# Scores of the bidirectional scan by pairs of heads, one sum of both directions ahead of the values, and an output-projection chunk asked for earlier

## The chip, the cores and the metric

The kernel runs on one core of one Trainium2 chip. The metric is the device time of one launch, in microseconds (us); lower is better. A core has a matrix engine (PE, with its weight loads shown apart as PEld), a vector engine (DVE), a scalar engine (ACT), GpSimd (POOL), and a queue engine (SP) that here does nothing but ask for transfers. They run on their own and meet at semaphores.

## The reference

Two layers (`DEPTH = 2`) over 256 latent tokens and 256 context tokens, 1024 wide. A layer has modulation vectors from two conditioning vectors, a normed and modulated input, one input projection whose columns feed four branches, one output projection, and then a mixture of 32 experts, two per token. All is float32. The branch that matters here is a gated linear attention with 4 heads (32 wide for queries and keys, 64 wide for values), in chunks of 64 tokens, once forward and once backward:

```python
def gla_chunked(q, k, v, log_a, s0):
    ...
    b = jnp.cumsum(log_a, axis=3)
    b_last = b[:, :, :, -1:, :]
    q_dec = q * jnp.exp(b)
    k_inv = k * jnp.exp(-b)
    mask = np.tril(np.ones((GLA_CHUNK, GLA_CHUNK), dtype=bool))
    scores = jnp.where(mask, jnp.einsum('bhnid,bhnjd->bhnij', q_dec, k_inv), 0.0)
    o_intra = jnp.einsum('bhnij,bhnjv->bhniv', scores, v)
    chunk_kv = jnp.einsum('bhnjd,bhnjv->bhndv', k * jnp.exp(b_last - b), v)
    ...
    o_inter = jnp.einsum('bhnid,nbhdv->bhniv', q_dec, s_in)
    return (o_intra + o_inter).reshape(bsz, nh, length, dv), s_final

def gla_bidir(q, k, v, la_f, la_b, s0_f, s0_b):
    o_f, s_f = gla_chunked(q, k, v, la_f, s0_f)
    rev = lambda t: jnp.flip(t, axis=2)
    o_b, s_b = gla_chunked(rev(q), rev(k), rev(v), rev(la_b), s0_b)
    return o_f + rev(o_b), s_f, s_b
```

The values `v` are the same for both directions, and the two outputs are added. In the last layer only the latent tokens go on after the scan.

## The kernel before

**Stages.** Each layer is written out once per engine. First the modulation products (`mod_product`, L1219), the norm, and the input projection with the local branches (L1259 to L1357); then the scan over token tiles of 128 (four tiles in layer 0, two in layer 1); then the router, and a loop over blocks of 32 tokens that stay with one expert (`expert`, L1584), while SP streams each expert's three chunks of 2 MB from memory (`refill`, L811).

**The scan stage.** `gla_steps` (L136) writes its order by hand, and PE, ACT and DVE all follow that list. For a tile `t` it has:
- `scores` (L1389): for each direction `d` one product, with `kiT` (the keys, 128 rows: 4 heads of 32, by 128 tokens) as the weights and `qbd` as the moving side. `qbd` is 128 x 512: the queries once per head with the rows of the other heads set to zero, which POOL writes (L917 to L924), a buffer for each direction, rewritten for the next tile once the scores of this tile are made.
- `masked` (L1838), on DVE: it reads the bank of each direction, multiplies by that direction's mask and writes `scm`.
- `outputs` (L1396): four products with the states (L1403), then for each direction and head one product of `scm` with the values (L1408), eight in all, summed in one bank. It waits once, for tile 0, on `s_S`: DVE signals that after `masked(0)` and the 14 steps of the state recurrence (L1852).
- `rows`, `ty` (L1382): norm and gate of the output, and its transpose.
- `pre` and `out` (`project_local`, `project_scan`; both through `product`, L1417): the output projection of the local branches and then of the scan's rows. `product` waits for both chunks of the projection weight, `wout` 0 and `wout` 1.

Every PE result goes through one of eight banks; `open_` (L1205) waits until the bank's last readers are done.

**The stream of weights.** `stream` (L259) is the list of 2 MB chunks that SP asks for in this order: `win` (input projection), `mod` (modulation), `wout`. `stream_slots` (L269) says which of four slots each goes to. Before each request SP waits for the landing of the chunk two places before it, and for the last use of what the slot held (L746 to L753), so a request that waits holds back every one behind it. Each `mod` chunk is used by one product of 16 matmuls.

Of the kernel before, what the change touches and what calls it, by code (L numbers as in the profile page):

```python
# [6 lines left out]
ALU = mybir.AluOpType  # L7
# [7 lines left out]
P = 128  # L15
D = 1024
KT = D // P
DEPTH = 2
# [7 lines left out]
HEADS = 4  # L26
DV = GROUP_W // HEADS
DK = DV // 2
# [43 lines left out]
def _const_layout():  # L72
    at = 0
    for name, n in (("ident", P), ("ones", P), ("before", P), ("cum_f", P), ("cum_b", P), ("after", P),
                    ("prev", P), ("sel", 2), ("heads", HEADS), ("eps", 1), ("chunks", 2),
                    ("tok1", TILES), ("qrow", 1), ("rev4", NG), ("rev32", NE), ("thr", 2 * 16), ("expert", 1),
                    ("before32", NE), ("slot", P), ("block", MAX_BLOCKS), ("inv", 2 * POOL_N)):
        CONST_COLS[name] = (at, n)
        at += n
    return at  # L80
# [6 lines left out]
def constants():  # L87

    c = np.zeros((P, CONST_N), np.float32)

    def put(name, v):
        a, n = CONST_COLS[name]
        c[:, a:a + n] = v

    j, i = np.arange(P)[:, None], np.arange(P)[None, :]
    same = (j // CHUNK) == (i // CHUNK)
    put("ident", j == i)
    put("ones", 1.0)
    put("before", j < i)
    put("cum_f", same & (j <= i))  # L100
    put("cum_b", same & (j >= i))
    put("after", same & (j > i))
    put("prev", same & (j < i))
    put("sel", (j % 32) == np.arange(2)[None, :])
    put("heads", (j // DK) == np.arange(HEADS)[None, :])
    put("eps", EPS)
    put("chunks", (j // CHUNK) == np.arange(2)[None, :])
    put("tok1", P * np.arange(TILES)[None, :] + j + 1)
    put("qrow", j // BLK - 4)
    put("rev4", NG - np.arange(NG)[None, :])  # L110
    put("rev32", NE - np.arange(NE)[None, :])
    thr = np.tile(BLK * np.arange(16.0), (P, 2, 1))
    thr[:, 0, 0] = -1.0
    thr[0:3, 1, 0] = -1.0
    put("thr", thr.reshape(P, 32))
    put("expert", j)
    put("before32", BLK * (j < np.arange(NE)[None, :]))
    put("slot", i % BLK)
    put("block", np.arange(MAX_BLOCKS)[None, :])
    inv = np.zeros((P, 2, POOL_N), np.float32)  # L120

    def counts(length, win):
        t = np.arange(length)
        return np.clip(t + win // 2, 0, length) - np.clip(t - win // 2, 0, length)

    for g, win in enumerate(WINDOWS):
        parts = slice(64 * (g % 2), 64 * (g % 2) + 64)
        for r in range(ROWS):
            inv[parts, g // 2, r * PX + PADW:r * PX + PADW + GRID_W] = 1.0 / counts(GRID_W, win)
        inv[parts, g // 2, POOL_X + PADW:POOL_X + PADW + CTX] = 1.0 / counts(CTX, win)  # L130
    put("inv", inv.reshape(P, -1))
    return c
# [126 lines left out]
def stream(l):  # L259

    keys = [(l, "mod", n) for n in range(4)] if l == 0 else []
    keys += [(l, "win", n) for n in (0, 1, 2, 4, 3)] + [(l, "mod", n) for n in range(4, 10)]
    keys += [(l, "wout", 0), (l, "wout", 1), (l, "mod", 10), (l, "mod", 11)]
    if l + 1 < DEPTH:
        keys += [(l + 1, "mod", n) for n in range(4)]
    return keys


def stream_slots(l):  # L269

    slots = [0, 1, 2, 3] if l == 0 else []
    slots += [0, 1, 2, 3, 0] + [1, 2, 1, 2, 3, 1]
    return slots + ([3, 1, 0, 2] + [0, 2, 0, 2] if l + 1 < DEPTH else [2, 1, 0, 3])


GROUPS = [(0, 1, 2), (3, 4, 5), (8, 6, 7)]
# [7 lines left out]
def build(nc, t_in, out):  # L284
    ctx = ExitStack()
    with ctx:
# [3 lines left out]
        def sem(name):  # L290
            return ctx.enter_context(nc.semaphore(name))
# [156 lines left out]
        s_qd = sem("decayed_qk_ready")  # L448
        s_S = sem("states_ready")
        s_qbd = sem("q_by_heads")  # L450
        s_y = sem("gla_rows_ready")
        s_res = sem("residual_added")
        s_ddh = sem("exp_input_ready")
# [381 lines left out]
        def _(pool):  # L835
# [13 lines left out]
            for l in range(DEPTH):  # L849
# [67 lines left out]
                for t in range(nt):  # L917
                    for d in range(2):
                        if t:
                            pool.wait_ge(made, jobs.at[(l, "score", t - 1, d)] + 1)  # L920
                        got(pool, "A", l, "tq", d)
                        pool.tensor_tensor(qbd[:, d, :].rearrange("p (h i) -> p h i", h=HEADS),
                                           bc(qdT[:, d, t * P:(t + 1) * P], 1, HEADS), bc(const("heads"), 2, P),
                                           ALU.mult).then_inc(s_qbd, 1)  # L924
                    if t == 0:
                        store_gates(2)
                    if t == 1:
                        load_gates()
                    if t == nt - 1:
                        store_gates(5)  # L930
                        load_expert_gates()
# [258 lines left out]
        def _(pe):  # L1190
# [57 lines left out]
            for l in range(DEPTH):  # L1248
# [138 lines left out]
                    ins.then_inc(made, 1)  # L1387

                def scores(t):  # L1389
                    for d in range(2):  # L1390
                        pe.wait_ge(s_qbd, 2 * (n_y + t) + d + 1)
                        bank = open_(l, "score", t, d)
                        mm(bank[:, :], kiT[:, d, t * P:(t + 1) * P], qbd[:, d, :], start=True,
                           stop=True).then_inc(made, 1)

                def outputs(t):  # L1396
                    if t == 0:
                        pe.wait_ge(s_S, l + 1)
                    bank = open_(l, "o", t)
                    for d in range(2):  # L1400
                        for par in range(2):
                            a = t * P + 64 * par
                            mm(bank[64 * par:64 * par + 64, 0:256], qdT[:, d, a:a + 64],  # L1403
                               state_in(d, 2 * t + par), start=d == 0, stop=False, skip_group_check=True)
                    for d in range(2):
                        got(pe, "D", l, "score", t, d)
                        for h in range(HEADS):
                            ins = mm(bank[:, DV * h:DV * (h + 1)], scm[:, d, h * P:(h + 1) * P],  # L1408
                                     qkvg[:, t, 256 + DV * h:256 + DV * (h + 1)], start=False,
                                     stop=d == 1, skip_group_check=True)  # L1410
                    ins.then_inc(made, 1)


# [230 lines left out]
        def _(dve):  # L1644
# [100 lines left out]
            for l in range(DEPTH):  # L1745
# [91 lines left out]
                got(dve, "D", l, "kv", 1, 1)  # L1837
                def masked(t):  # L1838

                    for d in range(2):  # L1840
                        bank = take(dve, l, "score", t, d)

                        mask = bc(const("cum_b" if d else "cum_f"), 1, HEADS)
                        ins = tt(scm[:, d, :].rearrange("p (h i) -> p h i", h=HEADS),
                                 bank[:, :].rearrange("p (h i) -> p h i", h=HEADS), mask, ALU.mult)
                        done(ins, "D", l, "score", t, d)

                masked(0)
                for n in range(1, NCH):
# [138 lines left out]
```

## Time and profile before

| | |
|---|---|
| median of 3 runs | 1449.41 us (1449.31 to 1453.82) |
| the profiled execution | 1445.59 us |
| its span | 1443.8 us |
| PE busy | 1188.2 us (82%), 12626 instructions |
| DVE busy | 583.7 us (40%) |
| ACT busy, POOL busy | 198.9 us (14%), 209.5 us (15%) |
| mean granted PE clock | 0.944 of full speed |
| transfers | 485.36 MB, mean 336 GB/s |

The span is the time between the first and the last event that the profiler recorded; the launch takes 1.8 us more. A busy share is a mean over stages that have different limits, so what an edit is worth is read from the chain of waits and from the stretch that it touches. A float32 matmul shows as two records, so an instruction count of the program is half of the count in the trace. In the trace a record's own duration overlaps its neighbours'; what a group of them takes is read from the start of its first to the start of what follows.

### The profile page before, as it was taken

To read this page: it belongs to the slowest core of one execution; us is meant where nothing else is said; L and a number is where in the kernel's file an instruction comes from. 1 tells how busy PE (TensorE), PEld (TensorE's weight loads), DVE (VectorE), ACT (ScalarE), POOL (GpSimd) and SP (SyncE) were. 2 spreads that over 40 slices of the span, in tenths; PEclk is the share of its full clock that TensorE was granted. 3 is DMA by queue.
4 is the path that set the end of the run, shared out by engine and by line. 5 is a ranking of instruction groups with operands and counts; after the bars stand their busy time and mean duration, and the time that the engine had idled before them with its cause. 6 is when DMAs were issued, how large, how long until landed. Compare 5 with 4: busy or idle time off the path is not lost.

```text
span 1443.8 us, 31287 instructions
## 1 busy us (share of the span) xinstructions
PE 1188.2 (82%) x12626; PEld 648.0 (45%) x12627; DVE 583.7 (40%) x1318; ACT 198.9 (14%) x422; POOL 209.5 (15%) x366
## 2 busy tenths in 40 slices
PE   3999999988989999776998799997888857666565
PEld 0445445454545554433554585544444433333332
DVE  1192153267767777544677551434111100100102
ACT  2103311240000000000000315122000000000001
POOL 4005021002111111111111011101111110110100
PEclk9999999999999999989999899998999987788987
DMA  9531564498999979999999736759999999999995
GB/s 350 195 117 59 204 256 160 175 400 309 423 420 417 421 306 421 417 422 420 417 420 419 282 128 222 290 228 368 394 419 375 419 421 417 422 419 420 422 417 236
DMA packets 99207, 485.36 MB, mean 336 GB/s; under 512 B 10247, under 2 KB 12851, under 8 KB 83170
## 3 DMA queue, kind: packets, MB, share of 16 engines
q1 hardware_dynamic: 90834, 469.96, 80.9%
q0 software_dynamic: 5712, 9.00, 1.8%
q10 hardware_dynamic: 2624, 5.89, 1.1%
q8 instruction: 26, 0.43, 0.1%
q14 instruction: 11, 0.09, 0.0%
HBM read 485.90 MB, written 4.23 MB: 339 GB/s over the span
## 4 chain that ended last, share of the span: by engine, by line
PE 50%; SPq 21%; DMA 17%; issue 4%; DVE 4%; ACT 3%; DVEq 0%; POOL 0%; ACTq 0%; POOLq 0%
SPq L780 20%; PE bank L1548 11%; PE bank L1265 9%; DMA ring<-in_expert_w_out 7%; PE bank L1573 6%; PE bank L1422 6%; PE bank L1563 5%; DMA work<-in_expert_w_out 5%; PE bank L1345 4%; PE bank L1225 2%; DMA ring<-in_w_mod 2%; DVE resid L1669 2%; ACT msb L1001 1%; DMA h_rows<-states 1%; PE bank L1554 1%
## 5 line engine op out<-in xcount | busy, mean ns | idle before, releaser
L1669 DVE TENSOR_TENSOR resid<-bank,resid 128x512 f32<-128x512 f32 x384 | 238.2, 683 | 124.6 <-PE bank L1573 124.6
L1548 PE MATMUL bank<-ring,msb 128*32 128x256 f32 x3456 | 226.4, 406 | 74.6 <-DMA ring<-in_expert_w_in 54.8
L1001 ACT ACTIVATE msb<-bank 128x256 f32<-128x256 f32 (+2 forms) x190 | 69.1, 364 | 909.8 <-PE bank L1548 817.8
L1548 PEld LDWEIGHTS bank<-ring,msb 128*32 128x32 f32 x3456 | 108.8, 115 | 182.6 <-DMA ring<-in_expert_w_in 71.7
L1563 PE MATMUL bank<-ring,msb 128*32 128x256 f32 x1728 | 112.8, 405 | 40.5 <-DMA ring<-in_expert_w_out 33.6
L1911 DVE COPY msb<-bank 128x256 f32<-128x256 f32 x85 | 35.7, 420 | 269.4 <-PE bank L1512 269.2
L962 POOL COPY work<-work 128x256 f32<-128x256 f32 x86 | 34.5, 401 | 689.9 <-issue 353.3
L1265 PE MATMUL bank<-actT,ring 128*128 128x512 f32 (+1 forms) x384 | 124.9, 487 | 1.0 <-ACT actT L1040 1.0
L1573 PE MATMUL bank<-work 32*128 32x256 f32 x1376 | 109.2, 436 | 4.4 <-DVE msb L1934 3.9
L952 POOL DMA_INDIRECT work<-h_rows,gidx x86 | 88.6, 1030 | 73.9 <-POOL gidx L949 73.9
L1548 PE MATMUL bank<-actT,msb 128*32 128x256 f32 x928 | 67.0, 438 | 34.9 <-DMA actT<-in_expert_w_in 28.3
L1265 PEld LDWEIGHTS bank<-actT,ring 128*128 128x128 f32 x384 | 72.4, 190 | 51.5 <-issue 46.2
L1563 PEld LDWEIGHTS bank<-ring,msb 128*32 128x32 f32 x1728 | 56.9, 114 | 84.5 <-issue 40.5
L1573 PEld LDWEIGHTS bank<-work 32*128 32x128 f32 x1376 | 68.6, 204 | 50.4 <-issue 34.7
L1563 PE MATMUL bank<-work,msb 128*32 128x256 f32 x928 | 60.7, 405 | 23.0 <-DMA work<-in_expert_w_out 18.2
L1934 DVE TENSOR_TENSOR work<-bank,egate 128x256 f32<-128x256 f32 x83 | 34.8, 420 | 103.7 <-PE bank L1563 102.8
L1225 PE MATMUL bank<-ring,csil 128*32 128x512 f32 x384 | 49.0, 649 | 22.9 <-DMA ring<-in_w_mod 22.9
L1422 PE MATMUL bank<-ring 128*128 128x512 f32 x144 | 63.2, 593 | 1.1 <-DMA ring<-in_w_out 1.1
L1548 PEld LDWEIGHTS bank<-actT,msb 128*32 128x32 f32 x928 | 32.1, 122 | 66.7 <-DMA actT<-in_expert_w_in 30.7
L1548 PE MATMUL bank<-states,msb 128*32 128x256 f32 x928 | 56.2, 382 | 5.2 <-DMA states<-in_expert_w_in 5.2
L1573 PE MATMUL bank<-msb,work 32*128 32x256 f32 x768 | 55.0, 400 | 2.6 <-DVE resid L1669 2.6
L1726 DVE SCALAR_TENSOR_TENSOR ring<-ring,chv 128x192 f32<-128x192 f32 (+20 forms) x144 | 55.0, 448 | 0.8
(254 smaller groups left out, 1078.2 us busy)
## 6 DMA issues: line engine op xcount, KB each, us to landing
ring<-in_expert_w_in SPq DMA_DIRECT2D x82, 2048.0 KB
ring<-in_expert_w_out SPq DMA_DIRECT2D x41, 2048.0 KB, 34.3
ring<-in_w_mod SPq DMA_DIRECT2D x24, 2048.0 KB, 12.5
actT<-in_expert_w_in SPq DMA_DIRECT2D x21, 2048.0 KB, 26.5
states<-in_expert_w_in SPq DMA_DIRECT2D x21, 2048.0 KB, 30.9
work<-in_expert_w_out SPq DMA_DIRECT2D x21, 2048.0 KB
ring<-in_w_in SPq DMA_DIRECT2D x8, 2048.0 KB, 11.2
ring<-in_w_out SPq DMA_DIRECT2D x4, 2048.0 KB, 13.3
```

The lines of the kernel that those rows point to most:

```text
L780: sp.dma_start(dst, src).then_inc(slot_ready[s], 16)
L952: pool.indirect_dma_start(out=xg[:, b, :], out_offset=None, in_=rows_h, in_offset=bass.IndirectOffsetOnAxis(ap=gidx[:, b:b + 1], axis=0), ...
L1001: return act.activation(o, i, func, **kw)
L1225: ins = mm(bank[g:g + 32, :], csil[:, k, :], w[:, k, :], start=k < 4, stop=k >= 4)
L1265: ins = mm(bank[:, 0:N], w[:, k, m * P:(m + 1) * P], aT[:, k, 0:N], start=k == 0, stop=k == KT - 1)
L1345: ins = mm(bank[:, a:512], aT[:, k, t * P:(t + 1) * P], w[:, k, a:512], start=k == 0, stop=k == KT - 1)
L1422: ins = mm(bank[:, :], branch[k][:, t * P:(t + 1) * P], w[:, k % 4, 512 * h:512 * h + 512], start=k == 4, stop=k == 1, skip_group_check=True)
L1548: ins = mm(PS[1][q, 0:256], xeT[:, c % 2, BLK * (c // 2):BLK * (c // 2 + 1)], w[:, k, 256 * g:256 * (g + 1)], start=c == 0, stop=c == KT - 1)
L1563: ins = mm(PS[3][q, 0:256], hT[:, k % 2, BLK * (k // 2):BLK * (k // 2 + 1)], w[:, k, 256 * g:256 * (g + 1)], start=k == 0, stop=k == 3)
L1573: ins = mm(PS[4 + g][:, 256 * j:256 * (j + 1)], sel[q, t * P:(t + 1) * P], ye[t // XT_TILES][q, :], start=start and j == 0, stop=True, ski ...
L1669: ins = tt(v, PS[4 + g].rearrange("p (t n) -> p t n", t=2), v, ALU.add)
L1726: yield lambda v=v, w=w, o=o: stt(v(dst, 0), v(src, o), w, v(dst, 0), ALU.mult, ALU.add)
```

## The change

Three things change.

1. **Scores by pairs of heads.** A new constant `pair` marks, for each of the 128 rows, which head of its pair it belongs to. POOL writes `qbd` as 128 x 256 per direction, not 128 x 512. PE multiplies rows 0 to 63 (heads 0 and 1) and rows 64 to 127 (heads 2 and 3) apart, each half with its own 64 rows of `kiT`. The two banks of a tile now hold one pair of heads each, with both directions side by side. Both banks are opened first, and both are signalled only after the second direction; POOL's wait for the buffer is for the last of them.
2. **One sum of both directions.** DVE masks the two banks as before, with an access pattern of one dimension more, then adds the two directions' masked scores (one 128 x 512 addition) and signals `s_both`. PE waits for that and makes four value products per tile, not eight.
3. **The order of the stream.** In layer 0 `wout` 0 is asked for ahead of `mod` 6 to 9, in layer 1 ahead of `mod` 8 and 9; `wout` 1 stays behind `mod` 9. The slots change so that `wout` 1 takes the slot of `mod` 8 and no longer that of `mod` 9, and `mod` 8 and `mod` 9 take the slots that `mod` 6 and `mod` 7 leave.

```diff
+    put("pair", (j // DK) % 2 == np.arange(2)[None, :])
...
-    keys += [(l, "win", n) for n in (0, 1, 2, 4, 3)] + [(l, "mod", n) for n in range(4, 10)]
-    keys += [(l, "wout", 0), (l, "wout", 1), (l, "mod", 10), (l, "mod", 11)]
+    keys += [(l, "win", n) for n in (0, 1, 2, 4, 3)] + [(l, "mod", 4), (l, "mod", 5)]
+    keys += [(l, "wout", 0)] * (l == 0) + [(l, "mod", 6), (l, "mod", 7)] + [(l, "wout", 0)] * (l > 0)
+    keys += [(l, "mod", 8), (l, "mod", 9), (l, "wout", 1), (l, "mod", 10), (l, "mod", 11)]
...
-    slots += [0, 1, 2, 3, 0] + [1, 2, 1, 2, 3, 1]
-    return slots + ([3, 1, 0, 2] + [0, 2, 0, 2] if l + 1 < DEPTH else [2, 1, 0, 3])
+    slots += [0, 1, 2, 3, 0] + ([1, 2, 3, 1, 2, 1, 2] if l == 0 else [1, 2, 1, 3, 2, 1, 3])
+    return slots + ([1, 0, 2] + [0, 2, 0, 2] if l + 1 < DEPTH else [1, 0, 3])
...
-                            pool.wait_ge(made, jobs.at[(l, "score", t - 1, d)] + 1)
+                            pool.wait_ge(made, jobs.at[(l, "score", t - 1, 1)] + 1)
                         got(pool, "A", l, "tq", d)
-                        pool.tensor_tensor(qbd[:, d, :].rearrange("p (h i) -> p h i", h=HEADS),
-                                           bc(qdT[:, d, t * P:(t + 1) * P], 1, HEADS), bc(const("heads"), 2, P),
+                        pool.tensor_tensor(qbd[:, d, 0:2 * P].rearrange("p (h i) -> p h i", h=2),
+                                           bc(qdT[:, d, t * P:(t + 1) * P], 1, 2), bc(const("pair"), 2, P),
                                            ALU.mult).then_inc(s_qbd, 1)
...
                 def scores(t):
+                    halves = [open_(l, "score", t, i) for i in range(2)]
                     for d in range(2):
                         pe.wait_ge(s_qbd, 2 * (n_y + t) + d + 1)
-                        bank = open_(l, "score", t, d)
-                        mm(bank[:, :], kiT[:, d, t * P:(t + 1) * P], qbd[:, d, :], start=True,
-                           stop=True).then_inc(made, 1)
+                        for i in range(2):
+                            ph = slice(64 * i, 64 * i + 64)
+                            ins = mm(halves[i][:, 2 * P * d:2 * P * (d + 1)], kiT[ph, d, t * P:(t + 1) * P],
+                                     qbd[ph, d, 0:2 * P], start=True, stop=True, skip_group_check=True)
+                            if d:
+                                ins.then_inc(made, 1)
...
-                    for d in range(2):
-                        got(pe, "D", l, "score", t, d)
-                        for h in range(HEADS):
-                            ins = mm(bank[:, DV * h:DV * (h + 1)], scm[:, d, h * P:(h + 1) * P],
-                                     qkvg[:, t, 256 + DV * h:256 + DV * (h + 1)], start=False,
-                                     stop=d == 1, skip_group_check=True)
+                    pe.wait_ge(s_both, n_y + t + 1)
+                    for h in range(HEADS):
+                        ins = mm(bank[:, DV * h:DV * (h + 1)], scm[:, 0, h * P:(h + 1) * P],
+                                 qkvg[:, t, 256 + DV * h:256 + DV * (h + 1)], start=False, stop=True,
+                                 skip_group_check=True)
...
-                    for d in range(2):
-                        bank = take(dve, l, "score", t, d)
-
-                        mask = bc(const("cum_b" if d else "cum_f"), 1, HEADS)
-                        ins = tt(scm[:, d, :].rearrange("p (h i) -> p h i", h=HEADS),
-                                 bank[:, :].rearrange("p (h i) -> p h i", h=HEADS), mask, ALU.mult)
-                        done(ins, "D", l, "score", t, d)
+                    a = CONST_COLS["cum_f"][0]
+                    mask = bc(cst[:, a:a + 2 * P].rearrange("p (d i) -> p d i", d=2), 2, 2)
+                    for i in range(2):
+                        bank = take(dve, l, "score", t, i)
+                        ins = tt(scm[:, :, 2 * P * i:2 * P * (i + 1)].rearrange("p d (h i) -> p d h i", h=2),
+                                 bank[:, :].rearrange("p (d h i) -> p d h i", d=2, h=2), mask, ALU.mult)
+                        done(ins, "D", l, "score", t, i)
+                    got(dve, "D", l, "score", t, 1)
+                    tt(scm[:, 0, :], scm[:, 0, :], scm[:, 1, :], ALU.add).then_inc(s_both, 1)
```

On PE, layer 0, from the products of keys and values (L1376 before, L1379 now) through the scores (L1393, L1398), the local projection (L1422, L1428), the states (L1403, L1410) and the values (L1408, L1414) of tile 0 and 1, with the scores of tile 2 between, the kernel before has:

```order
L1376 MATMUL bank<-work 128x256 x16
L1393 MATMUL bank<-ring 128x512 x4
L1422 MATMUL bank<-ring 128x512 x12
L1403 MATMUL bank<-states,ring 64x256 x4
L1408 MATMUL bank<-work,ring 128x64 x8
L1225 MATMUL bank<-ring,csil 32x512 x16
L1393 MATMUL bank<-ring 128x512 x2
L1403 MATMUL bank<-states,ring 64x256 x4
L1408 MATMUL bank<-work,ring 128x64 x8
```

The changed kernel has, at the same place:

```order
L1379 MATMUL bank<-work 128x256 x16
L1398 MATMUL bank<-ring 128x256 x8
L1428 MATMUL bank<-ring 128x512 x12
L1410 MATMUL bank<-states,ring 64x256 x4
L1414 MATMUL bank<-work,ring 128x64 x4
L1228 MATMUL bank<-ring,csil 32x512 x16
L1398 MATMUL bank<-ring 128x256 x4
L1410 MATMUL bank<-states,ring 64x256 x4
L1414 MATMUL bank<-work,ring 128x64 x4
```

No row changes its place; the scores are twice as many of half the width, and the value products half as many.

On SP, layer 0, the requests for the input projection (`in_w_in`), modulation and output projection before were:

```order
L770 DMA ring<-in_w_in 128x8x512 x3
L770 DMA ring<-in_w_in 128x8x288
L770 DMA ring<-in_w_in 128x8x512
L770 DMA ring<-in_w_mod 128x8x512 x6
L770 DMA ring<-in_w_out 128x4x1024 x2
L770 DMA ring<-in_w_mod 128x8x512 x6
L780 DMA ring<-in_expert_w_in 128x4096 x2
```

In the changed kernel they are:

```order
L773 DMA ring<-in_w_in 128x8x512 x3
L773 DMA ring<-in_w_in 128x8x288
L773 DMA ring<-in_w_in 128x8x512
L773 DMA ring<-in_w_mod 128x8x512 x2
L773 DMA ring<-in_w_out 128x4x1024
L773 DMA ring<-in_w_mod 128x8x512 x4
L773 DMA ring<-in_w_out 128x4x1024
L773 DMA ring<-in_w_mod 128x8x512 x6
L783 DMA ring<-in_expert_w_in 128x4096 x2
```

One of the two `in_w_out` requests has gone ahead of four `in_w_mod` requests, and the other stands where it stood.

## Rows read from the trace of the kernel before

**Rows 1.** The page's chain that ended last: shares of the span by line

```profile
SPq L780 20%; PE bank L1548 11%; PE bank L1265 9%; DMA ring<-in_expert_w_out 7%; PE bank L1573 6%; PE bank L1422 6%; PE bank L1563 5%; DMA work<-in_expert_w_out 5%; PE bank L1345 4%; PE bank L1225 2%; DMA ring<-in_w_mod 2%; DVE resid L1669 2%; ACT msb L1001 1%; DMA h_rows<-states 1%; PE bank L1554 1%
```

**Rows 2.** The chain, layer 0's scan: start us, us, what

```profile
224.84 1.92 PE bank L1393 x4
226.75 1.01 PE bank L1403 x8
227.77 1.93 PE bank L1408 x16
...
276.13 12.03 PE bank L1422 x28
```

**Rows 3.** Stretches: length, busy per engine, PE clock, DMA share, GB/s

```profile
340.00:345.00 5.00, 4.86 (x76) 2.78 (x68) 3.11 (x6) 0.66 (x2) 0.58 (x2) 1.00 0.32 75
...
520.00:530.00 10.00, 8.66 (x140) 4.66 (x136) 7.66 (x16) 0.66 (x2) 1.61 (x3) 1.00 0.48 184
...
964.00:968.00 4.00, 4.00 (x11) 1.85 (x10) 2.77 (x4) 0.23 (x1) 0.00 (x0) 1.00 0.24 90
```

**Rows 4.** Timeline, layer 0: start us, us, engine, line; in brackets idle, releaser

```profile
198.55 3.83 PE L1376 MATMUL bank<-work 64*128 64x256 f32 x32
...
199.78 5.39 DVE L1833 TENSOR_TENSOR states<-bank,cst 128x256 f32<-128x256 f32 x16 [1.35 <-PE bank L1376]
...
202.30 1.98 PE L1393 MATMUL bank<-ring 128*128 128x512 f32 x4
...
203.52 2.03 POOL L922 TENSOR_TENSOR ring<-ring,cst 128x512 f32<-128x512 f32 x2 [2.88 <-PE bank L1393]
...
204.61 2.13 PE L1393 MATMUL bank<-ring 128*128 128x512 f32 x4 [0.32 <-POOL ring L922]
...
205.20 1.29 DVE L1844 TENSOR_TENSOR ring<-bank,cst 128x512 f32<-128x512 f32 x2
...
206.41 8.61 DVE L1852 SCALAR_TENSOR_TENSOR states<-states,small 128x256 f32<-128x256 f32 x14
...
207.79 10.54 PE L1422 MATMUL bank<-ring 128*128 128x512 f32 x24 [1.05 <-DMA ring<-in_w_out]
```

**Rows 5.** SP's requests, layers 0 and 1; last, L770's times from request to landing

```profile
194.24 0.39 SPq L770 DMA_DIRECT2D ring<-in_w_out  x1
...
904.00 0.54 SPq L770 DMA_DIRECT2D ring<-in_w_mod  x1
...
920.68 0.37 SPq L770 DMA_DIRECT2D ring<-in_w_out  x1
...
929.83 0.55 SPq L770 DMA_DIRECT2D ring<-in_w_mod  x1
...
DMA to landing us min/median/max: 9.3/12.8/14.0
```

**Rows 6.** Timeline, layer 1

```profile
916.93 3.64 PE L1225 MATMUL bank<-ring,csil 128*32 128x512 f32 x32
...
927.03 1.98 PE L1393 MATMUL bank<-ring 128*128 128x512 f32 x4
...
929.34 2.12 PE L1393 MATMUL bank<-ring 128*128 128x512 f32 x4 [0.32 <-POOL ring L922]
...
931.14 6.37 DVE L1852 SCALAR_TENSOR_TENSOR states<-states,small 128x256 f32<-128x256 f32 x14
931.30 10.46 PE L1422 MATMUL bank<-ring 128*128 128x512 f32 x24
```

**Rows 7.** Groups by line and shape: count, busy us, mean ns, idle before

```profile
L1822 DVE TENSOR_TENSOR work<-work 128x512 f32<-128x512 f32 x2 | 1.4, 684 | 0.0
...
L913 POOL TENSOR_TENSOR states<-states,cst 64x256 f32<-64x256 f32 x12 | 8.7, 728 | 0.9
```

**Rows 8.** The page's granted PE clock, in tenths, in 40 slices of 36.1 us

```profile
PEclk9999999999999999989999899998999987788987
```

More of the change, by code:

```diff
@@ L74, in _const_layout @@
     for name, n in (("ident", P), ("ones", P), ("before", P), ("cum_f", P), ("cum_b", P), ("after", P),
-                    ("prev", P), ("sel", 2), ("heads", HEADS), ("eps", 1), ("chunks", 2),
+                    ("prev", P), ("sel", 2), ("heads", HEADS), ("pair", 2), ("eps", 1), ("chunks", 2),
                     ("tok1", TILES), ("qrow", 1), ("rev4", NG), ("rev32", NE), ("thr", 2 * 16), ("expert", 1),
@@ L450, in build @@
         s_qbd = sem("q_by_heads")
+        s_both = sem("masked_scores_of_both_directions")
         s_y = sem("gla_rows_ready")
```

## The prediction

> **What bounds the kernel now.** I read the chain that ended last first, because busy shares say nothing of which stage a shorter product helps. By line [rows 1] it is mostly the expert loops (L780, L1548, L1573, L1563, the expert transfers); the lines that the change touches are small in it. Then I read the same chain in order of time inside layer 0's scan [rows 2]: scores, states, values and projection of every tile stand in it as PE work, one behind the other, without a wait of another engine between them. So PE is the bound of that stage, and a microsecond less of PE there moves its end by one.
>
> Does it move the end of the kernel? The expert loops behind the scan are held by transfers for long stretches, and a stage held by bandwidth could swallow an earlier start. Three stretches speak against that [rows 3]: at 340 to 345 us, ahead of layer 0's loop, the transfers fill 0.32 of their time, at 520 to 530 inside it 0.48, at 964 to 968, ahead of layer 1's loop, 0.24. In each the queue waits for PE to free a buffer, so everything behind hangs on PE's progress and moves with it.
>
> Then the timeline at the start of the scan, where other engines come near [rows 4]. PE works through L1376 until the scores begin at 202.30, pauses 0.32 us for POOL's `qbd`, ends the scores at 204.61 + 2.13 = 206.74 and waits 1.05 us for the projection weight. The local projection ends at 207.79 + 10.54 = 218.33. DVE ends the state steps at 206.41 + 8.61 = 215.02, so PE arrives 3.3 us later than the states it needs.
>
> **The scores.** Per tile before: 4 records, 1.92 us [rows 2], 0.48 each. Now 8 records of 256 columns on 64 rows. A row of exactly that shape exists: L1376, 64*128 by 256 columns, 32 records from 198.55 to the start of the scores at 202.30 [rows 4], 0.117 us each. Eight take 0.94 us. There, as in the new scores, the two row halves write different banks. A record of 256 columns in turn would take half of 0.48, so two halves of the rows evidently run side by side there. Bounds: 0.94 us, and 1.92 us with no overlap, where nothing is saved. I take 1.04, as the exposed first weight load may stay: 0.88 us saved per tile.
>
> The Trainium skill has this rule in "TensorE: Matmul & The Clock Gate", Part 3 (Packing small matmuls): a matmul on few rows takes as long as one on all 128, and the gain comes only from tiles in other row groups that run at the same time. By that rule the trace's 0.117 us is overlap and not a shorter product; where the two halves failed to overlap here, the scores would save nothing, which is rival A.
>
> **The values.** 16 records, 1.93 us per tile [rows 2]; eight go: 0.97 us saved per tile. The weights are as wide as before, so a record stays 0.12 us.
>
> **POOL.** `qbd` halves from 1.02 us per direction (2 in 2.03, [rows 4]). Bounds: unchanged 1.02, and half of it, 0.51; the nearest row with as many columns is 0.73 [rows 7], on 64 rows. I take 0.62. For tiles 2 and 3 POOL is early anyway.
>
> **DVE.** Per tile one addition of 128x512 more, 0.68 us by L1822 [rows 7]; the masks keep their element count, 0.65 each (2 in 1.29, [rows 4]). Bounds for the extra dimension: nothing, or twice that. Who waits: for tile 0, the state steps are queued behind the addition, and PE waits for them. For the later tiles the mask starts when the previous tile's output bank is made, and PE does the scores (0.94) and states (1.01), and after tile 0 two modulation products as well, before it needs the sum. That is 5.5 us of cover for tile 1 in layer 0, against 1.29 + 0.70 = 2.0 needed; in layer 1, without scores between, 4.6 us. For tiles 2 and 3 a whole projection lies between. So the addition is hidden everywhere but at tile 0, even with masks twice as dear.
>
> **The stream.** Before, the second projection chunk was asked for only when `mod` 9 had been used; the first at 194.24, and PE waited until 207.79 for both [rows 4, 5]. Now the first comes long before, and the second is asked when `mod` 8 has been used, at about 194.2. With a 2 MB request close behind it, such a chunk took from 920.68 to 929.83 = 9.15 us in layer 1, since the request at 929.83 waits for just that landing [rows 5]. So it is there at 203.4, ahead of PE. Bound: the longest landing of the line, 14.0 [rows 5], 208.2. In layer 1 it is asked when `mod` 8 is used, at 916.93 + 1.8 = 918.8 [rows 6], and is there at 927.9. The price of the new order is that `mod` 8 and 9 are asked late: in layer 1 at 904.0 and 905.7, when `mod` 6 and 7 have been used [rows 5], where before `mod` 9 and the first projection chunk were. PE wants them at 916.93 and 918.7. At the median landing, 12.8 [rows 5], `mod` 8 comes at 916.8 and `mod` 9 at 918.5, just in time; at 14.0 each is 1.0 us late. I take zero.
>
> **The sum, layer 0.** Scores of tile 0 end at 203.3; POOL starts as before at 203.52 and writes the two halves by 204.1 and 204.8; PE ends the second direction at 205.3. The local projection then ends at 205.3 + 10.54 = 215.85. DVE: 206.41 + 0.70 + 8.61 = 215.72. PE and DVE arrive together, and the states start at 215.9, not at 218.33: 2.4 us. Were the masks twice as dear, DVE would take over here, 1.3 us later. Then 4 values and 2 scores (tiles 2 and 3): 4 x 0.97 + 2 x 0.88 = 5.6. Layer 0: 8.0 us.
>
> **Layer 1** [rows 6]. POOL's second tile ended its first half at 929.34 after starting at 928.3. Now the halves are there at 928.9 and 929.5, and the scores end at 930.0 and not at 929.34 + 2.12 = 931.46: 1.4 us. The projection ends at 940.5; DVE at 931.14 + 0.70 + 6.37 = 938.2, in time. Two values: 1.9. Layer 1: 3.3 us.
>
> Together 11.4 us. The profiled execution took 1445.59 us, of which 1443.8 are the span and 1.8 lie around it; it would take 1434.2. The median shown, 1449.41, lies 3.8 us above that execution; taking the gain off it gives 1438.0.
>
> **Rivals.**
> A. The row halves do not overlap. For it: the new order alternates halves, where L1376 has two of a half in a row; against: the shape is the same and its row is clear. The scores of tile 0 then end at 204.2, of tile 1 at 206.7, and the states start at 217.25. Gains: 1.1 + 3.9 in layer 0, 0.1 + 1.9 in layer 1, 7.0 us: 1442.4.
> B. The second projection chunk lands late, because `mod` 10 is asked right behind it and shares the bandwidth. At 14.0 us it costs the 2.4 of layer 0 and 0.3 more, and in layer 1 PE waits until 932.8, 1.3 later than before: 5.6 - 0.3 + 1.9 - 1.3 = 5.9 us: 1443.5. Against: the 9.15 us measured in just that neighbourhood.
> C. Layer 0's gain is swallowed in its expert loop, which is fed by transfers for most of its length; only layer 1's 3.3 us are left: 1446.1. Against: the three gaps [rows 3].
> D. The other side: the expert loops meet a lower granted clock. The page shows 7 tenths in two slices where most have 9 [rows 8]; a shift of the blocks against their transfers could put such a slice where PE is the bound. One slice of 36.1 us, PE 0.9 busy, at 0.7 instead of 0.95: 36.1 x 0.9 x (0.95/0.7 - 1) = 11.6 us, as much as the gain; from the second one on it is slower. Two: 23.2 - 11.4 = 11.8 us slower, 1461. Against: nothing is added in those stages and the scan's pauses get shorter.
>
> **How the numbers follow.** Forecast 0.74, A 0.09, B 0.06, C 0.07, D 0.04. About 0.3%, 4.3 us, is what a measurement of this kernel can tell from no change. The forecast, A and B are beyond it; C lies within, and with small variants of it within has 0.09; faster 0.88, slower 0.03. The likeliest case's own range is 9 to 13 us of gain (13: halves fully overlapped, POOL at half; 9: masks twice as dear and `mod` 8 and 9 late). With 1 or 2 us for where the median falls among runs that spread by 4, the range is 1434.5 to 1443.5, which takes in A and nearly B.
>
> **What would show it.** In the trace after: the scores of a tile in about 1.0 us and 8 records, the values in 0.97 and 8 records; the local projection of tile 0 starting near 205.3, the states near 215.9 with PE waiting for DVE by a few tenths; no wait of L1228 for a modulation chunk, and none of L1428 for the projection's; layer 0's scan about 8 us and layer 1's 3.3 us shorter, and the last gaps of the transfers shifted by as much. I am wrong if the scores still take 1.9 us, if L1428 or L1228 waits on a transfer, or if the expert loops begin 8 us earlier and end at the old time.

## The result, and the profile after

The changed kernel takes 1438.4 us (median of 7 runs, 1435.06 to 1445.77); the kernel before, run beside it, 1449.93 us (1448.45 to 1453.82). The ratio is 0.9924, 95% interval 0.9907 to 0.9941: 11.0 us less, between 8.5 and 13.5. The forecast was 1438.0 us and 11.4 us less. A second measurement of the same kernel gave 0.9927 (0.9903 to 0.9951).

The chain that ended last has the same lines after the change, first of all the request line (L783 now, L780 before), and no line of the scan has grown [rows 1]:

```profile
SPq L783 20%; PE bank L1554 11%; PE bank L1268 9%; DMA ring<-in_expert_w_out 7%; PE bank L1579 6%; PE bank L1428 6%; PE bank L1569 5%; PE bank L1348 4%; PE bank L1228 2%; DMA work<-in_expert_w_out 2%; DMA ring<-in_w_mod 2%; DMA actT<-in_expert_w_in 2%; DVE resid L1675 2%; ACT msb L1004 2%; PE bank L1560 1%
```

In the profiled execution the key-value products of layer 0 began at 201.48 us, and before at 198.55 [rows 4]. Only the first transfers lie between; other profiles of these kernels have any start from 198.6 to 202.2 there. So the spans (1443.8, now 1436.6) understate the gain, and everything below counts from those products. Here is the timeline of layer 0's scan after the change (start us, us, engine, line), against [rows 4]:

```profile
201.48 3.83 PE L1379 MATMUL bank<-work 64*128 64x256 f32 x32
...
205.04 1.13 PE L1398 MATMUL bank<-ring 64*128 64x256 f32 x8
206.27 1.17 POOL L925 TENSOR_TENSOR ring<-ring,cst 128x256 f32<-128x256 f32 x2 [3.12 <-PE bank L1398]
207.02 1.18 PE L1398 MATMUL bank<-ring 64*128 64x256 f32 x8 [0.84 <-POOL ring L925]
208.13 10.57 PE L1428 MATMUL bank<-ring 128*128 128x512 f32 x24
208.14 1.29 DVE L1850 TENSOR_TENSOR ring<-bank,cst 128x512 f32<-128x512 f32 x2
...
209.47 0.98 DVE L1854 TENSOR_TENSOR ring<-ring 128x512 f32<-128x512 f32 x1
...
210.37 7.08 DVE L1860 SCALAR_TENSOR_TENSOR states<-states,small 128x256 f32<-128x256 f32 x14
218.63 1.08 PE L1410 MATMUL bank<-states,ring 128*64 128x256 f32 x8
219.64 1.10 PE L1414 MATMUL bank<-work,ring 128*128 128x64 f32 x8
220.68 3.64 PE L1228 MATMUL bank<-ring,csil 128*32 128x512 f32 x32
...
224.25 1.14 PE L1398 MATMUL bank<-ring 64*128 64x256 f32 x8
...
225.31 1.08 PE L1410 MATMUL bank<-states,ring 128*64 128x256 f32 x8
...
226.32 1.10 PE L1414 MATMUL bank<-work,ring 128*128 128x64 f32 x8
227.27 1.04 PE L1237 MATMUL bank<-cst,msb 128*128 128x128 f32 x8
```

The scores of tile 2 now run from 224.25 to the states at 225.31: 1.06 us. Before they took 1.91 us read the same way, and 1.92 by the chain [rows 2]. The values run from 226.32 to 227.27. PE waits 0.84 us for POOL ahead of the scores of tile 1, then no more for the projection chunk. DVE ends the state steps at 217.45, and PE begins the states at 218.63. The projection chunk was asked for at 197.17, and the request at 205.26 waits for its landing (8.1 us), well ahead of 208.13:

```profile
197.17 0.38 SPq L773 DMA_DIRECT2D ring<-in_w_out  x1
...
205.26 0.54 SPq L773 DMA_DIRECT2D ring<-in_w_mod  x1
```

What PE waited for between 100 and 300 us after the change (total us, times, longest): no transfer, neither a modulation chunk nor one of the projection, and no `s_both`:

```profile
PE bank L1247 <- ACT work L1036: 1.5, 1, 1.5
PE bank L1303 <- ACT zT L1004: 1.2, 1, 1.2
PE bank L1463 <- ACT work L1004: 1.1, 1, 1.1
PE bank L1398 <- POOL ring L925: 0.8, 1, 0.8
PE bank L1457 <- ACT actT L1043: 0.5, 1, 0.5
```

Layer 1 after, against [rows 6]:

```profile
919.22 3.83 PE L1379 MATMUL bank<-work 64*128 64x256 f32 x32
...
922.78 1.13 PE L1398 MATMUL bank<-ring 64*128 64x256 f32 x8
...
924.75 1.18 PE L1398 MATMUL bank<-ring 64*128 64x256 f32 x8 [0.84 <-POOL ring L925]
925.87 10.57 PE L1428 MATMUL bank<-ring 128*128 128x512 f32 x24
...
927.82 6.38 DVE L1860 SCALAR_TENSOR_TENSOR states<-states,small 128x256 f32<-128x256 f32 x14
936.36 1.08 PE L1410 MATMUL bank<-states,ring 128*64 128x256 f32 x8
```

The table puts all kernels beside each other: each number is the distance in us from the first key-value product of that layer to the first product of the step, read from PE's timeline. "Scan end" is the first transpose after the last output projection, "layer 1" is the distance between the key-value products of the two layers, "loop" is the time from the first block of an expert loop to the first product of the next input projection, or to the end.

```
                     layer 0                        loop 0  layer 1  layer 1's own                  loop 1
                     project.  states  scan end                      project.  states  scan end
before                 9.24    19.71    89.44       502.4   724.72    8.03     18.42    47.49       446.1
after                  6.65    17.15    81.81       503.0   717.74    6.65     17.14    44.42       446.0
after, again           6.65    17.14    81.80       503.1   717.76    6.65     17.15    44.42       446.2
x1 old stream          9.60    21.77    86.42       503.0   722.15    6.64     17.14    44.42       447.4
x2 no sum              6.65    17.15    85.38       503.6   721.89    6.65     17.14    46.21       447.7
x3 full scores         8.02    18.42    84.58       502.2   721.03    8.02     18.42    45.70       449.0
x12 the same again     8.02    18.41    84.57       501.1   718.86    8.02     18.42    45.69       447.2
x7 layer 1 only        8.03    18.42    88.15       501.8   724.03    6.64     17.14    44.42       447.2
x10 stream alone       8.03    18.42    88.15       502.3   724.83    8.03     18.42    47.49       448.5
x4 two buffers         5.49    16.74    81.40       503.2   717.43    5.49     15.99    43.26       447.4
x9 the same, POOL late 5.49    15.99    80.64       499.2   714.33    5.48     15.98    43.26       446.1
```

The distances in the scans repeat within 0.02 us in the two kernels that were profiled twice (after, and x3 with x12); what stands behind a wait for a transfer (before, x1) comes from one profile each. The loops vary by some 2 us between executions of one kernel, and between 499 and 504, 446 and 449 over all. So the scan columns tell what an edit does, and the totals whether it arrives. From before to after, layer 0's scan is 7.63 us shorter and layer 1's 3.07: 10.7 us, against 11.0 (8.5 to 13.5) in the total. Of layer 0's 7.63, 6.98 have arrived at layer 1's key-value products.

### The profile page after: what moved, and what is told of

It reads as the page before. It is cut to its first block, busy times and chain, and to the rows that moved or that the text cites. A ratio compares the mean times of both kernels' runs of the same rounds, so it can differ in the third digit from the quotient of the medians.

```text
span 1436.6 us, 31242 instructions
## 1 busy us (share of the span) xinstructions
PE 1183.7 (82%) x12602; PEld 647.8 (45%) x12603; DVE 586.3 (41%) x1324; ACT 198.9 (14%) x422; POOL 203.9 (14%) x366
## 4 chain that ended last, share of the span: by engine, by line
PE 50%; SPq 22%; DMA 15%; issue 4%; DVE 4%; ACT 3%; POOL 0%; DVEq 0%; ACTq 0%; POOLq 0%
SPq L783 20%; PE bank L1554 11%; PE bank L1268 9%; DMA ring<-in_expert_w_out 7%; PE bank L1579 6%; PE bank L1428 6%; PE bank L1569 5%; PE bank L1348 4%; PE bank L1228 2%; DMA work<-in_expert_w_out 2%; DMA ring<-in_w_mod 2%; DMA actT<-in_expert_w_in 2%; DVE resid L1675 2%; ACT msb L1004 2%; PE bank L1560 1%
## 5 line engine op out<-in xcount | busy, mean ns | idle before, releaser
L1428 PE MATMUL bank<-ring 128*128 128x512 f32 x144 | 63.3, 594 | 0.0
```

Of the source, the lines that this page charges most:

```text
L1428: ins = mm(bank[:, :], branch[k][:, t * P:(t + 1) * P], w[:, k % 4, 512 * h:512 * h + 512], start=k == 4, stop=k == 1, skip_group_check=True)
```

## Experiments

**x1: the old stream.** The scores by pairs and the sum stay.

```diff
-    keys += [(l, "wout", 0)] * (l == 0) + [(l, "mod", 6), (l, "mod", 7)] + [(l, "wout", 0)] * (l > 0)
-    keys += [(l, "mod", 8), (l, "mod", 9), (l, "wout", 1), (l, "mod", 10), (l, "mod", 11)]
+    keys += [(l, "mod", n) for n in range(6, 10)]
+    keys += [(l, "wout", 0), (l, "wout", 1), (l, "mod", 10), (l, "mod", 11)]
```

> The changed kernel with the old order and slots of the stream. Theory (PE is the bound in the scan, each part is worth what it takes off PE): in layer 0 the projection L1428 starts 9.2 us after the key-value products L1379 begin, as before the change, where the changed kernel has 6.7, with a wait for the projection chunk of about 2.5 us; in layer 1 it stays at 6.7, since the chunk landed 6.6 us after that point before the change. Total 2.5 us above the changed kernel, about 1441. Rival 1 (the stream's order is most of the gain): 8 us above, about 1446. Rival 2 (it does nothing, the chunk would have come in time): the time of the changed kernel, 1438.4.

Measured: ratio to before 0.9963 (0.9947 to 0.9979), 5.6 us above the changed kernel; by the table 4.6 us of that stand in layer 0's scan, none in layer 1's. The wait was 2.89 us, where about 2.5 was expected. But the projection behind it took 12.23 us, not 10.57:

```profile
207.70 1.18 PE L1397 MATMUL bank<-ring 64*128 64x256 f32 x8 [0.84 <-POOL ring L924]
...
211.77 12.23 PE L1427 MATMUL bank<-ring 128*128 128x512 f32 x24 [2.89 <-DMA ring<-in_w_out]
```

The stretches of 2 us there (length, busy per engine, granted PE clock, DMA share, GB/s):

```profile
210.00:212.00 2.00, 0.23 (x1) 0.26 (x2) 1.96 (x4) 0.00 (x0) 1.32 (x2) 1.00 1.04 390
212.00:214.00 2.00, 2.00 (x4) 0.82 (x4) 1.89 (x5) 0.00 (x0) 0.00 (x0) 0.63 1.07 412
214.00:216.00 2.00, 2.00 (x3) 0.73 (x3) 1.93 (x5) 0.00 (x0) 0.00 (x0) 0.52 1.05 422
216.00:218.00 2.00, 2.00 (x6) 0.93 (x5) 1.46 (x4) 0.00 (x0) 0.00 (x0) 1.00 0.97 366
```

After the pause the granted clock is 0.63 and 0.52 for 4 us, that is mostly the lower of its two levels, and PE makes three records in 2 us where it else makes six. Four us at a mean of 0.575 lose 1.7 us, and the projection is 1.66 us longer. The 1.05 us wait of the kernel before had no such dip, nor had one of 1.14 us in x8, further down: 10.54 us are the undisturbed length in both [rows 4]. So the wait was priced nearly rightly and its consequence was missed. This dip stands in one profile. The total's interval (some 2 to 9 us above the changed kernel) excludes rival 2, but neither the expected 2.5 us nor rival 1's 8; it is the scan's 4.6 us that lies between them.

**x10: the stream alone**, the same edit the other way, on the kernel before.

```diff
-    keys += [(l, "wout", 0), (l, "wout", 1), (l, "mod", 10), (l, "mod", 11)]
+    keys += [(l, "wout", 0)] * (l == 0) + [(l, "mod", 6), (l, "mod", 7)] + [(l, "wout", 0)] * (l > 0)
+    keys += [(l, "mod", 8), (l, "mod", 9), (l, "wout", 1), (l, "mod", 10), (l, "mod", 11)]
```

> The kernel before with the new order and slots of the stream alone. Theory: PE's wait of 1.05 us for the projection chunk in layer 0 goes and nothing else changes: the projection starts 8.2 us after the key-value products begin, not 9.24, in layer 0, and 8.03 in layer 1 as before. Rival (the modulation chunks asked later make PE wait): a wait at a modulation product in either layer.

The projection starts at 8.03 in layer 0 (9.24 before), in layer 1 nothing changes, and PE waits for no modulation chunk. One run, 1449.67 us. The stream alone is worth 1.3 us in the scan; with the shorter scores it is worth 4.6. The two parts are not additive: the shorter the scores, the longer PE would stand at the chunk that the old order brings.

**x2: no sum.** Pair scores and new stream stay; eight value products.

```diff
-                    pe.wait_ge(s_both, n_y + t + 1)
-                    for h in range(HEADS):
+                    got(pe, "D", l, "score", t, 1)
+                    for d in range(2):
+                        for h in range(HEADS):
...
-                    tt(scm[:, 0, :], scm[:, 0, :], scm[:, 1, :], ALU.add).then_inc(s_both, 1)
```

> The changed kernel without the addition of both directions: eight value products per tile, no addition on DVE. Theory: the values take 1.8 us per tile and not 0.9, so 0.9 x 6 tiles = 5.4 us above the changed kernel, about 1443.8. Rival (the addition on DVE costs on the path what it saves on PE, since the states of tile 0 wait behind it): about 3.6 us above, as the addition's 0.7 to 1.0 us would come back once per layer; PE would start the states of tile 0 earlier than in the changed kernel, counted from L1379.

By the table the states start at 17.15 and 17.14 with or without the addition, so DVE's extra work costs the path nothing, and the rival falls. The scans are 3.57 us (four tiles) and 1.79 us (two tiles) longer: 0.89 us per tile. Ratio 0.998 (0.9964 to 0.9996), 8.1 us above the changed kernel, where the scans explain 5.4.

**x3 and x12: full scores**, with the sum and the new stream, the same kernel twice.

```diff
-                             ins = mm(halves[i][:, 2 * P * d:2 * P * (d + 1)], kiT[ph, d, t * P:(t + 1) * P],
-                                     qbd[ph, d, 0:2 * P], start=True, stop=True, skip_group_check=True)
+                        mm(bank[:, :], kiT[:, d, t * P:(t + 1) * P], qbd[:, d, :], start=True,
+                           stop=True).then_inc(made, 1)
```

> The changed kernel with the scores as before the change (128 rows by 512 columns per direction, queries written by head, one mask per direction), the sum and the new stream kept. Theory: scores 1.9 us per tile, POOL 1.04 us per direction; the projection L1428 starts 8.2 us after L1379 begins in both layers, not 6.7, and tiles 2 and 3 lose 0.85 us each: 1.5 + 1.5 + 1.7 = 4.7 us above the changed kernel, about 1443.1. Rival (the gain of the shorter scores lies in POOL's shorter write alone): 0.9 us per layer, 1440.2, with tiles 2 and 3 unchanged.

> The kernel of x3 (full scores, with the sum and the new stream) once more. Its total lay 6.5 us above the changed kernel, its two scans only 4.1; in its profile layer 1's expert loop took 449.0 us from the first block to the end, the changed kernel's 446.0 and 446.2 in two profiles. Theory (the loops' length varies between executions whatever the kernel): another value between 446 and 449 here, and a total about 4.1 us above the changed kernel, ratio about 0.9953. Rival (the loop's length belongs to the kernel, by how its blocks meet the transfers): 449.0 within 0.3 us and a ratio about 0.9969 again.

The projection starts at 8.02 in both layers; the scans are 2.77 and 1.28 us longer, 4.05 us in all, where 4.7 was expected. Tiles 2 and 3 lose 1.5 us together, so the rival (only POOL's write matters) falls. The first total was 0.9969 (0.9957 to 0.9981), the second 0.9951 (0.9935 to 0.9968), the latter 3.9 us above the changed kernel, as the scans say. In the profiles loop 1 took 449.0 and 447.2 us, loop 0 502.2 and 501.1, with the scans alike. So 1.8 us of that loop vary between executions of the same kernel; that a smaller part belongs to the kernel is not excluded, as the changed kernel had 446.0 and 446.2.

**x5: both halves on the same rows** (heads 2 and 3 get the scores of heads 0 and 1).

```diff
-                            ph = slice(64 * i, 64 * i + 64)
+                            ph = slice(0, 64)
```

> The changed kernel with both score halves taken from rows 0 to 63, so heads 2 and 3 get the scores of heads 0 and 1; the number, shape and banks of the products stay. Theory (the shorter scores come from two row halves at work side by side): without different rows they run in turn, eight records of about 0.21 us, 1.7 to 1.9 us per tile and not 1.06. Rival (a product on 64 rows is shorter by itself): 1.06 us per tile, unchanged.

The number, shape and banks of the records are the same, and the scores of tile 2 take 1.92 us again, from their start to that of the states:

```profile
223.94 1.99 PE L1398 MATMUL bank<-ring 64*128 64x256 f32 x8
225.86 1.08 PE L1410 MATMUL bank<-states,ring 128*64 128x256 f32 x8
```

So the gain is the overlap of two row halves, and rival A of the prediction names its condition rightly. (The total, one run of 1494.72 us, is not comparable: its loops took 513 and 488 us, since, as far as can be told, other scores route the tokens to experts otherwise.)

**x7: layer 1 only.** Layer 0 has scores, masks and values of before; the stream is new in both.

```diff
+                scores = scores_new if l else scores_old
...
+                masked = masked_new if l else masked_old
```

> Layer 0's scores, masks and values as before the change, layer 1's as changed, the new stream in both. Theory (each layer's gain reaches the end): layer 0's scan is shorter by the chunk's wait alone, 1.0 to 1.2 us, layer 1's by 3.1 us: 4.2 us below the kernel before, 1445.2. Rival (layer 0's gain is swallowed by its expert loop): the time of the changed kernel plus little, 1439.

The scans are as expected, 1.29 and 3.07 us shorter than before. Ratio 0.9991 (0.9973 to 1.0009): between 3.9 us faster and 1.3 slower. The expected 4.2 us lie just outside, and so do the 4.4 of its own scans; the rival's 1439 us lies far outside. What layer 0's two parts add in the scan is 6.34 us. Of these, 6.29 have arrived at layer 1's key-value products (724.03 against 717.74 in the table), and in the totals they show as 9.7 us, with an uncertainty of some 3.6: layer 0's gain does reach the end.

**x6 and x8: POOL later**, on the changed kernel and on the one before.

```diff
                 for t in range(nt):
+                    if t == 2:
+                        pool.wait_ge(s_S, l + 1)
                     for d in range(2):
```

> The changed kernel with POOL waiting for the end of the state steps before it writes the queries of tile 2. Theory (DVE's addition at 0.98 us and a state step of 0.83 us in layer 0 are DVE held up by POOL's writes beside it): the addition takes 0.69 us and the 14 state steps 6.4 us, as in layer 1, in place of 7.1; the scan is no shorter, since PE comes 1.2 us after DVE there. Rival (the long ones are DVE's own waits, for a bank or a transfer): unchanged at 0.98 and 7.1 us.

> The kernel before, with POOL waiting for the end of the state steps before it writes the queries of tile 2. Theory: the one state step of 2.7 us in layer 0 becomes 0.48 us like the others, the 14 steps take 6.4 us and not 8.6; the scan is no shorter, PE was 3.3 us behind. Rival: 8.6 us as before.

In x6 the addition and the state steps take:

```profile
209.60 0.69 DVE L1856 TENSOR_TENSOR ring<-ring 128x512 f32<-128x512 f32 x1
210.21 6.38 DVE L1862 SCALAR_TENSOR_TENSOR states<-states,small 128x256 f32<-128x256 f32 x14
```

In x8 the state steps, with POOL's two writes for tile 2 moved behind them:

```profile
209.71 6.37 DVE L1854 SCALAR_TENSOR_TENSOR states<-states,small 128x256 f32<-128x256 f32 x14
...
216.23 2.04 POOL L924 TENSOR_TENSOR ring<-ring,cst 128x512 f32<-128x512 f32 x2 [6.09 <-DVEq L1856]
```

Both as the theory had it; the scan's length does not change (81.81 in x6, 89.53 in x8). The single runs took 1442.09 and 1451.28 us.

**x4: two query buffers**, so that POOL writes tile 1 without waiting.

```diff
-                            pool.wait_ge(made, jobs.at[(l, "score", t - 1, 1)] + 1)
+                            pool.wait_ge(made, jobs.at[(l, "score", t - 2, 1)] + 1)
...
+                        b = 2 * P * (t % 2)
+                        pool.tensor_tensor(qbd[:, d, b:b + 2 * P].rearrange("p (h i) -> p h i", h=2),
```

> The changed kernel with the free half of the query buffer used for every second tile, so that POOL writes tile 1 without waiting for the scores of tile 0. Theory: PE's 0.84 us wait for POOL goes in both layers and the scan ends 0.8 to 0.9 us earlier in each, 1.7 us in all, about 1436.7, if DVE still ends the states first (it was 1.2 us ahead of PE in layer 0 and 2.2 us in layer 1). Rival (two POOL writes more beside DVE's reads of the key-value banks hold DVE up): DVE ends later, PE waits for the states in layer 0, and the gain is 0.8 us or none.

Measured: ratio 0.9922 (0.9901 to 0.9943). Layer 1 gains 1.16 us, more than the 0.84 us of the wait: the 16 score records of tiles 0 and 1 now follow each other in 1.93 us from their start to the projection, where they took 3.09 us with the wait between them. Layer 0 gains 1.16 at the projection, but only 0.41 at the states: there POOL's four writes run beside DVE, and PE waits 0.69 us for it. DVE, POOL and PE of x4:

```profile
207.38 3.37 POOL L926 TENSOR_TENSOR ring<-ring,cst 128x256 f32<-128x256 f32 x4
207.96 7.67 DVE L1861 SCALAR_TENSOR_TENSOR states<-states,small 128x256 f32<-128x256 f32 x14
215.73 1.08 PE L1411 MATMUL bank<-states,ring 128*64 128x256 f32 x8 [0.69 <-DVEq L1863]
```

The rival was right on layer 0, though by another pair of writes than it named: those of tiles 2 and 3, beside the state steps.

**x9: x4 with POOL held until the state steps end** (the edit of x6).

> The changed kernel with two query buffers, and POOL's writes for tile 2 held until the state steps end. Theory: with the buffers alone the scores of tile 1 lost their wait (the projection starts 5.5 us after L1379 begins, not 6.65) but DVE, slowed beside POOL, ended the states only 16.7 us after it; here DVE ends in time and the states start at 16.0 in both layers: 1.15 us less than the changed kernel in each, 2.3 in all, about 1436 against 1438.4. Rival (POOL's later writes make the scores of tile 2 wait): the values of tile 1 start later and the gain is lost.

POOL writes at 213.87, the states start at 15.99 and 15.98 in the two layers:

```profile
213.87 2.32 POOL L928 TENSOR_TENSOR ring<-ring,cst 128x256 f32<-128x256 f32 x4 [7.36 <-DVEq L1865]
214.74 1.08 PE L1413 MATMUL bank<-states,ring 128*64 128x256 f32 x8
```

Both scans are 1.16 us shorter than the changed kernel's, as expected. Ratio 0.9907 (0.9876 to 0.9939), 1436.29 us, beside 0.9927 (0.9903 to 0.9951), 1440.59 us, for the changed kernel on the same chip. It is the shortest version by the traces; the totals cannot tell 2.3 us.

**x11: the changed kernel once more**, without an edit.

> The changed kernel once more, as the measure for x9 on the same chip. Theory: ratio to before of 0.9924 within its interval, and the same distances from L1379 in the scan; only the start of the first transfers and the length of the expert loops vary between executions, by some 3 us each. Rival (the stage distances vary too): differences above 0.3 us in them.

0.9927, and the scan distances agree within 0.02 us.

## Why the prediction was right

- **PE bounds the scan, and its microseconds arrive.** Right: 10.7 us taken off the two scans, 11.0 measured, and x7 excludes that layer 0's loop swallows its gain (rival C). Of the three stretches that were called up for it [rows 3], the first was placed wrongly: 340 to 345 us is inside layer 0's loop, whose first block PE began at 318.61 us. Its transfers are still as little busy as was said.
- **Scores.** Predicted 1.04 us per tile, measured 1.06; saved 0.85 in tile 2 (1.91 before) and 0.74 in tile 3, whose scores took 1.81 before: 0.88 was taken for both. The shape's own row [rows 4] was the right source, and x5 shows the mechanism.
- **Values.** 0.97 us per tile predicted, 0.89 measured. Half of the group's 1.93 us was taken, but a group does not halve with its records. Read from its start to that of the next step, it took 1.84 us for 16 records and takes 0.94 for eight (in tile 0, ahead of the modulation product, 1.93 and 1.04). Eight records are worth 0.89 to 0.90 us, and the rest stays with the group.
- **Start of layer 0's scan.** Predicted: projection 205.3 on the clock of before, states 2.4 us earlier. Measured 205.2 (198.55 + 6.65) and 2.56. POOL's write took 0.59 us where 0.62 was taken. But PE and DVE were to arrive together, and DVE came 1.2 us ahead. The 8.61 us of state steps [rows 4] were taken as the work of 14 steps; they held one step of 2.7 us, stopped by POOL. With half as much POOL work it shrank to 7.08, which paid for the longer addition (0.98, not 0.68).
- **Layer 1.** Projection 1.4 predicted, 1.38 measured; DVE early, as foreseen; scan 3.3 against 3.07.
- **The stream.** A `mod` chunk is used by 8 matmuls, which are 16 records, and not by 16 matmuls as the description of the stream has it; the prediction's 1.8 us per chunk is right, and what it calls two products is one group of 32 records. The chunk landed in 8.1 us where 9.15 was taken, in both layers without a wait (rival B, whose 0.3 us beyond the old start would by its own landing at 208.2 be 0.4), and no modulation chunk was late. What the prediction missed is how much hung on it: the sum had the end of the 1.05 us wait as a small term, but without the new order the wait grows to 2.89 us, and a stretch at a lower clock follows it (x1).
- **Rival A** did not come about; **rival D** did not: the mean granted clock is 0.938 in the first profile and 0.943 in the second, against 0.944 before, and loop 1 took 446.0 and 446.2 against 446.1.
- **Luck.** The scans give 10.7 us where 11.4 was added up (8.0 and 3.3, before rounding); the values alone make 0.5 us of that, six times 0.08. The total cannot show so little: its interval is 5 us wide. That 1438.0 was forecast and 1438.4 measured is closer than the terms were.

Open: the totals of x1, x2, x3 and x7 lie 1 to 3 us above what their scans say, within or near their intervals. x12 shows such an excess go away in a second measurement of x3; the others were not repeated.

## What to carry to other kernels

Price a new matmul shape from a row of the same shape, read from its start to that of the next step, and ask what makes that row short: here it was two row halves at work at once, which the same products on one half do not have. When a chain on one engine is shortened, move up the transfer it meets next in the same edit: taken alone it looked worth 1.3 us, and behind the shortened chain it was worth 4.6. Of these, 2.95 us are the later start of the projection, and 1.66 the slower stretch of TensorE that followed the longer pause. And before a group's time is used as a term, look at its longest member.

## What the runs showed of the hardware

A step of DVE can stand while POOL works, and in a trace this looks like one long instruction in a uniform group. In the kernel before, the 28 state steps had these durations (ns, min/median/max), and POOL wrote the queries of tile 2 beside the first of them, which began at 206.41:

```profile
L1852 DVE SCALAR_TENSOR_TENSOR states<-states,small x28: 474/480/2712, 206.4 to 937.0; 128x256 f32<-128x256 f32 x28
```

```profile
206.78 2.05 POOL L922 TENSOR_TENSOR ring<-ring,cst 128x512 f32<-128x512 f32 x2
```

With POOL's writes moved behind them (x8):

```profile
L1854 DVE SCALAR_TENSOR_TENSOR states<-states,small x28: 476/480/485, 209.7 to 941.5; 128x256 f32<-128x256 f32 x28
```

In the changed kernel the same meeting cost both engines something. On DVE the addition took 0.98 us (0.69 in x6) and two state steps 0.83 each; on POOL the two writes took 1.11 and 0.78 us (0.60 each in x6):

```profile
209.80 1.86 POOL L925 TENSOR_TENSOR ring<-ring,cst 128x256 f32<-128x256 f32 x2
```

The Trainium skill says in "SBUF — State Buffer", section "Who interferes with whom", that DVE and GpSimd share a pair of ports under an exclusive lock, and that a DVE instruction with two inputs in SBUF contends with a GpSimd instruction that reads SBUF. The traces agree for the state step and for the addition, which read two tensors of SBUF. A mask, which reads one bank and one tensor of SBUF, took 0.69 us beside POOL's write at 204.52 in the kernel before, and as long without one. The same section says that the order of issue decides who is blocked. The starts in these traces do not show that order: the long state step began 0.37 us ahead of POOL's first write (206.41 against 206.78), the long addition 0.33 us (209.47 against 209.80), and both were held up all the same.
